# GpSimd subtracts low parts of weights in several pieces, and the planner's durations are refitted

## What is computed

```python
# layer 0: one input projection feeds two head groups
qa, ka, va, ga, qs, ks, vs, gs = split_cols(x @ w_in, EVEN_SPLITS)
# (A) 4 heads, differential attention: two softmax maps with a distance penalty
w = p[:, :, 0] - lam * p[:, :, 1]
# (B) 8 heads, stick-breaking attention
log_skip = jnp.where(earlier, jax.nn.log_sigmoid(-z), 0.0)
log_pass = lax.cumsum(log_skip, axis=3, reverse=True) - log_skip
a = jnp.where(earlier, jnp.exp(jax.nn.log_sigmoid(z) + log_pass), 0.0)
y = jnp.concatenate([ya, ys], axis=-1) @ w_out      # both gated by silu
# layer 1: (C) 8 heads of latent attention, low-rank q and kv, rotary part, gated, one output projection
# after each layer
h = layer_norm(ALPHA * h + y, ln_g[i], ln_b[i])
```

## Time and profile before

| what | value |
|---|---|
| median of 3 timed runs | 1339.77 us (1339.58 to 1344.28) |
| the profiled execution's own time | 1342.14 us |
| its span, first to last instruction | 1340.2 us |
| TensorE busy | 1294.9 us, 97% |
| VectorE busy | 871.3 us, 65% |
| ScalarE busy | 565.2 us, 42% |
| GpSimd busy | 477.1 us, 36%, 461 instructions |

### The profile page before, as it was taken

The page is one execution under the profiler, slowest core; times in us unless marked ns, Lnnn a source line. Parts: engine busy times, 40 slices in busy tenths (PEclk is TensorE's granted clock), DMA queues, the critical chain, the costliest instruction groups (busy, mean ns, idle before and its releaser), DMA issues.

```text
span 1340.2 us, 22174 instructions
## 1 busy us (share of the span) xinstructions
PE 1294.9 (97%) x8228; PEld 1221.5 (91%) x8228; DVE 871.3 (65%) x1959; ACT 565.2 (42%) x1332; POOL 477.1 (36%) x461
## 2 busy tenths in 40 slices
PE   8999999999999999998999999998999999999997
PEld 7999998999899999997888999998999989998886
DVE  5685868586677848669555323654778677776455
ACT  3444646364744535356101012533565545656200
POOL 3323221233224142246533324563333234334531
PEclk9999999999999999998999999999999999999999
DMA  6001010101010111214233311122111112115242
GB/s 227 33 28 36 17 49 32 49 33 48 33 40 25 37 45 52 63 29 137 68 126 126 111 32 61 66 83 75 36 48 45 48 44 64 41 46 194 69 161 79
DMA packets 46922, 88.25 MB, mean 66 GB/s; under 512 B 4048, under 2 KB 29648, under 8 KB 46688
## 3 DMA queue, kind: packets, MB, share of 16 engines
q1 hardware_dynamic: 44368, 78.45, 17.8%
q10 hardware_dynamic: 2448, 8.39, 1.6%
HBM read 66.84 MB, written 19.98 MB: 65 GB/s over the span
## 4 chain that ended last, share of the span: by engine, by line
PE 82%; DVE 9%; ACT 5%; issue 2%; POOL 1%; DMA 1%; DVEq 0%; SPq 0%; ACTq 0%; POOLq 0%
PE bank L2023 41%; PE bank L2174 13%; PE bank L2091 11%; PE bank L2146 8%; PE bank L2113 6%; DVE ring L1808 2%; DVE pb L1790 1%; PE bank L2062 1%; PE bank L2131 1%; ACT rtmp L1390 1%; DVE big L1607 1%; PE bank L2196 1%; DVE big L1847 1%; DVE tb L1737 1%; ACT vtok L1426 1%
## 5 line engine op out<-in xcount | busy, mean ns | idle before, releaser
L2023 PE MATMUL bank<-big,wsp 128*128 128x344 f32 (+2 forms) x3024 | 550.4, 327 | 8.4 <-DVE big L1607 4.5
L2023 PEld LDWEIGHTS bank<-big,wsp 128*128 128x128 f32 x3024 | 481.1, 189 | 15.0 <-POOL wsp L1067 4.2
L1066 POOL TENSOR_SCALAR wsp<-wraw 128x1024 fp32r<-128x1024 f32 (+4 forms) x92 | 84.3, 917 | 529.7 <-PE bank L2023 414.9
L1808 DVE TENSOR_TENSOR ring<-bank,ring 128x512 fp32r<-128x512 f32 (+3 forms) x280 | 154.9, 569 | 71.6 <-ACT ring L1477 44.8
L2174 PE MATMUL bank<-big,wsp 128*128 128x512 f32 x800 | 191.5, 397 | 1.5 <-DVE big L1847 1.2
L2174 PEld LDWEIGHTS bank<-big,wsp 128*128 128x128 f32 x800 | 149.3, 188 | 36.4 <-DVE big L1847 1.7
L1067 POOL TENSOR_TENSOR wsp<-wraw,wsp 128x1024 fp32r<-128x1024 f32 (+4 forms) x92 | 179.3, 1949 | 7.7
L2023 PE MATMUL bank<-h1t,wsp 128*128 128x344 f32 (+2 forms) x1080 | 173.9, 322 | 1.4 <-DVE lraw L1655 1.4
L2023 PEld LDWEIGHTS bank<-h1t,wsp 128*128 128x128 f32 x1080 | 170.2, 188 | 3.6 <-DVE lraw L1655 1.7
L1477 ACT ACTIVATE ring<-bank 128x512 fp32r<-128x512 f32 (+1 forms) x200 | 106.0, 555 | 112.8 <-PE bank L2113 80.4
L2146 PE MATMUL bank<-ring,vtok 128*128 128x256 f32 (+1 forms) x1040 | 143.3, 279 | 2.0 <-DVE ring L1808 1.0
(11 more groups left out here) (138 smaller groups left out, 1497.6 us busy)
## 6 DMA issues: line engine op xcount, KB each, us to landing
wraw<-in_w SPq DMA_DIRECT2D x47, 512.0 KB, 3.4
wraw<-y_scratch SPq DMA_DIRECT2D x17, 448.0 KB, 3.8
woraw<-in_wo SPq DMA_DIRECT2D x12, 512.0 KB, 5.3
y_scratch<-ot SPq DMA_DIRECT2D x37, 128.0 KB, 1.7
xres<-in_x SPq DMA_DIRECT2D x8, 512.0 KB, 4.7
h_scratch<-res ACTq DMA_DIRECT2D x8, 512.0 KB, 2.6
gate_scratch<-gtmp SPq DMA_DIRECT2D x8, 512.0 KB, 2.9
gate<-gate_scratch SPq DMA_DIRECT2D x8, 512.0 KB, 3.7
```

The source lines that it names most:

```text
L1066: pool.wait_ge(S["pool_step"], tick(nc.gpsimd.tensor_scalar(hi, raw, 1.0, 1.0, ALU.mult, ALU.mult)))
L1808: V.tensor_tensor(to, bank[T_BANK[t]][from_, 0:w], lo_hi(R[from_, r % NRING, 0, 0:w]), ALU.subtract)\
L2023: ins = mm(dst, wsp[:, SLOT[kind, u], a, k, :], rhs[:, b, k0 + k, c0:c0 + w], start=(k == 0 and a == 0 and b == 0), stop=last)
```

## The change

The subtraction in `split` gets a number of parts: as many as half the number of 128-column blocks of a weight tile, so 4 for 8 blocks, 3 for 7 (of 3, 3 and 1 blocks), 2 for 4 and 1 for 2. Nothing waits between the parts; the last one signals. The subtraction in GpSimd's `out_weight` goes in four parts of 256 columns. Other callers of `split` (latents, the last block of an output) keep one. In the planner, durations of the combination of kind A, of the scan of kind B, of products with a 128-column block, of GpSimd's split of a weight and of both kinds of low parts of output weights get other figures. Nothing else is edited.

```diff
@@ weave(layer)
             if kind == "A":
-                L.put("dve", "C", ("C", t), 1.9 * n_all + 1000, [("act", ("E", t, 1)), emptied(g)], 90)
+                L.put("dve", "C", ("C", t), 1.77 * n_all + 850, [("act", ("E", t, 1)), emptied(g)], 90)
...
             else:
-                L.put("dve", "C", ("C", t), 2.4 * n_all, [("act", s), emptied(g)], 90)
+                L.put("dve", "C", ("C", t), 2.15 * n_all + 60, [("act", s), emptied(g)], 90)
...
-            L.put("pe", "X", x, (1 if tiles == [0] else 2 if kind == "B" else 3) * (0.4545 * cols + 1.5 * len(tiles)),
+            L.put("pe", "X", x, (1 if tiles == [0] else 2 if kind == "B" else 3)
+                  * (pe_ns(cols) if tiles == [0] else sum(pe_ns(256) if tile <= pair_of(blocks)[0] + 1 else 83 for tile in tiles)),
...
-        L.put("pool", "W", ("W", n), 385 * kt + 450, ([("sp", ("LW", n))] if n >= first_w + 2 else []) + done, 20)
+        L.put("pool", "W", ("W", n), 385 * kt + 450 + 70 * (kt // 2 - 1), ([("sp", ("LW", n))] if n >= first_w + 2 else []) + done, 20)
...
-            L.put("dve", "W", wo, 2300, [("act", wo)], 90)
+            L.put("dve", "W", wo, 1700, [("act", wo)], 90)
         else:
-            L.put("pool", "O", wo, 2700, [("act", wo)], 20)
+            L.put("pool", "O", wo, 2800, [("act", wo)], 20)
@@ GpSimd
-            def split(hi, lo, raw):
+            def split(hi, lo, raw, parts=1):
 
                 pool.wait_ge(S["pool_step"], tick(nc.gpsimd.tensor_scalar(hi, raw, 1.0, 1.0, ALU.mult, ALU.mult)))
-                return nc.gpsimd.tensor_tensor(lo, raw, lo_hi(hi), ALU.subtract)
+                size = -(-raw.shape[1] // parts)
+                for a in range(0, raw.shape[1], size):
+                    b = min(a + size, raw.shape[1])
+                    ins = nc.gpsimd.tensor_tensor(lo[:, a:b], raw[:, a:b], lo_hi(hi[:, a:b]), ALU.subtract)
+                return ins
...
-                        ins = split(wsp[:, i % 2, 0, 0:kt, :], wsp[:, i % 2, 1, 0:kt, :], from_)
+                        ins = split(wsp[:, i % 2, 0, 0:kt, :], wsp[:, i % 2, 1, 0:kt, :], from_, max(kt // 2, 1))
...
-                nc.gpsimd.tensor_tensor(wok[:, 1, k, :], raw_out(layer, k), lo_hi(wok[:, 0, k, :]), ALU.subtract)\
-                    .then_inc(S["wo_split_pool"], 1)
+                for a in range(0, D, D // 4):
+                    part = slice(a, a + D // 4)
+                    ins = nc.gpsimd.tensor_tensor(wok[:, 1, k, part], raw_out(layer, k)[:, part], lo_hi(wok[:, 0, k, part]),
+                                                  ALU.subtract)
+                ins.then_inc(S["wo_split_pool"], 1)
```

## The result

The changed kernel takes 1354.05 us (median of 4 runs, 1352.45 to 1354.86) where the one before took 1340.02 in the same comparison: ratio 1.0097, 95% interval 1.0077 to 1.0116. I had forecast 1334.5. The profiled execution took 1352.45 us, with a span of 1350.5; it is the shortest of the four, while the profiled one of the kernel before (1342.14) is 2.1 us above its median, so the two profiles are 10.3 us apart where the medians are 14.0 apart.

A forecast was written before the change was run, and what follows sets the result against it. TensorE, busy 97%, was taken to bound the kernel. Terms -7.6 + 1.0 + 0.2 + 1.0 + 0.2 + 0 = -5.2 us gave 1336.9 profiled, 1334.5 us as median; range 1326 to 1345.

The forecast's parts named there:

- The bound: Whole kernel: TensorE, busy 97% of 1340.2 us, bounds it; 22 us idle in two attention stretches is the most to win.
- Pieces let VectorE in: At GpSimd's weight subtractions: a held VectorE step waits at most one piece, 0.77 us, where held 1.5 to 2.1 before.
- the waits on the combining: TensorE's waits on VectorE's combining of kind A (L1781): forecast to be gone.
- The price a piece: On GpSimd: 0.19 us for each of 218 more instructions, 41 us more busy time, near 518 us in all.
- The gain of -7.6: At TensorE's waits on held VectorE steps: three quarters of 10.1 us won, range 0 to -10.1.
- all eleven waits: TensorE waits from 55.92 to 1244.24 us whose last link is a VectorE step held by a GpSimd subtraction, 10.1 us.
- What GpSimd loses, +1.0 + 0.2 + 1.0: GpSimd's queue: query copies near 512 later +1.0, a 512-column weight in layer 1 +0.2, output weights +1.0 (0 to +2.9).
- my rival: Starved GpSimd, stick-breaking units: each piece waits out a scan, a subtraction needs 7 to 9 us; +8, 1348 us, chance 0.15.
- The start: First weight in pieces: TensorE starts 2.4 us later, then loses 2.2 us of later waits; net +0.2.
- the +0.2: Net cost in us forecast for the kernel's start, between -1.4 and +2.4.
- The refit, taken as 0 between -7 and +7: Planner's new durations alter only the order; effect taken as 0, bounded by a third of 22 us idle either way.
- -5.2: Sum of all forecast terms in us, on the profiled execution of 1342.14 us.

The follow-up runs named there:

- E1: Changed kernel with all planner durations, so the engines' order, as before and the pieces kept; 1347.18 us against 1342.26 for the kernel before, ratio 1.0040.
- the old order's three: Kernels alike in kind A's part: the one before, one with new planner figures in layer 1 only, one with the scan figure alone; idle 29.4, 27.5, 28.2 us.
- E2: Changed kernel with the new planner durations but every subtraction whole as before; 1355.68 us, ratio 1.0102.
- G2: Changed kernel with the planner's old duration for products put back (59.7 ns for 128 columns); 1354.45 us, ratio 1.0087.
- H1: Kernel before, whole subtractions, with only the planner's figure for combining of kind A refitted; 1351.99 us against 1341.70, ratio 1.0076.
- H1 to H4: Kernel before with planner figures changed: combining alone 1.0076, kind B's scan alone 1.0021, 128-column products alone 1.0020, VectorE's and TensorE's refits mirrored 1.0110.
- G4: Kernel before, no pieces, with old planner durations in layer 0 and the new ones in layer 1; 1340.06 us, ratio 0.9992.
- J1: Old planner durations in layer 0, new in layer 1; pieces for kind A's weights but the first and layer 1's attention and output; 1333.88 us against 1339.56, ratio 0.9951.
- G3: Old planner durations in layer 0, new in layer 1, and pieces only for kind A's weights but the first; 1338.21 us, ratio 0.9977.
- E3: Changed kernel with five early output-projection matmuls of layer 0 moved behind the turn of group 46, tile pair 1; 1351.69 us, ratio 1.0069.

## Why the prediction was wrong

**The bound** was read rightly: TensorE's idle time explains every kernel's span.

**Pieces let VectorE in**: right. The held step of 53 us, the cast of 810 and the scans' mean (2618 to 2464) came out as forecast. But the waits on the combining, which were to be gone, are 5.9 us where they were 2.5. The price a piece was too high: four back to back with nothing between take 2.84 us (at 26.31) where one takes 2.39, so 0.15 us for each further one and not 0.19; GpSimd is busy 533 us and not 518, and what was added (56 us) beyond 218 x 0.15 = 33 I take for waiting on VectorE, as the 6.14 us row shows it.

**The gain of -7.6** stood for all eleven waits. In kind A's part 3 to 4.5 us of it came, in either order (E1 against the old order's three, the change against E2: 32.6 and 37.1; G2 against H1: 36.0 and 39.1). In kind B's part it was more than eaten, and in layer 1 it came only with the new order.

**What GpSimd loses, +1.0 + 0.2 + 1.0**, is the first term that failed: in the old order the pieces cost 6.8 us net in kind B's part (E1). I had put +1.0 on query copies at one place (512) and +1.0 (0 to 2.9) on output weights; in that part the waits for these grew by 2.0 and 4.4 us, and those for weights, which I had at nothing there, by 2.5. It isn't my rival either, by which each piece waits out a scan and a subtraction needs 7 to 9 us: a 1024-column one takes 3.49 on average there and 4.8 at most. The sum of the pieces is +4.1 us of span where I had -5.2.

**The start** did no harm that shows: TensorE starts 1.5 us later (2.4 was expected) and loses its later waits. At the first turn of values the change (41.0 us) and E1 (40.4) are even ahead of the kernel before (41.7), but other kernels with whole subtractions are there at 39.0 to 40.4, so the +0.2 is neither shown nor refuted.
```profile
5.41 4.72 POOL L1071 TENSOR_TENSOR wsp<-wraw,wsp 128x256 fp32r<-128x256 f32 x4
...
10.18 10.33 PE L2031 MATMUL bank<-big,wsp 128*128 128x352 f32 x48 [4.23 <-POOL wsp L1071]
```

**The refit, taken as 0 between -7 and +7**, is the step that broke the forecast: by itself it is +13.0 us of span (E2; +13.7 by its ratio), outside its bounds. I bounded it by the idle time that was there, which bounds a gain only; a loss has no such bound. And I took it as equally likely to help or to hurt. H1 to H4 show that four orders near the old one, refitted or refitted backwards, are all slower in layer 0 taken whole. That fits an old order which happens to suit this chip better than its planner knows; why it does isn't settled, and four orders are few. That the new combining figure puts eight turns too early is seen (H1), not why the planner's picture is off there: in the change the combining before the wait at 225.45 itself took 2.0 us, less than the figure's 2.24 for its 784 keys.

**Their sum** is less than their parts: 4.1 and 13.0 give 17.1, the change has 10.3. By parts of the table, kind A's adds up (-4.5 and +7.7 against +3.2); the two overlap in kind B's, where +6.8 and +5.8 give +9.4, and in layer 1, where +1.3 and -0.5 give -2.9.

**TensorE's clock** is a rival that I left out: the same matmuls take longer where the granted clock is 0.50 (see the last section), and the change has 13.7 us at that clock in kind B's part, the kernel before 6.8. It doesn't explain the loss there by itself: with the same order and whole subtractions G4 has 3.4 us at 0.50 in this part, the kernel before and J1 6.8 and G3 10.2, and all four have 25.8 to 25.9 us of idle time. For the change, E1 (13.7 too) and E3 (17.1), no run separates the clock from the waits; nor does one in kind A's part.

## What to carry to other kernels

An order written by a planner is data that was matched to the chip: a change of its durations needs its own experiment, whatever it does for the fit of one instruction. Idle time bounds what a new order can gain, not what it can lose. Cutting a long instruction that blocks another engine pays where the blocked engine's work is short and waited for, and costs where that engine often has long work ready and its own result is waited for, since a piece may then wait out such an instruction; decide it stage by stage, with the idle time of equal work as the measure. A single large wait in the trace (8.9 us here) may hide others behind it: moving it brought 4 at most.

## What the runs showed of the hardware

GpSimd subtractions of 256 columns with no wait between them are recorded at 0.74 to 0.75 us each and 0.70 apart when nothing hinders them (four in 2.84 us), where one of 1024 takes 2.39, so most of the fixed cost of some 0.2 us stays. A waiting VectorE instruction of two SBUF inputs gets in at a boundary between two: in the change, three of them took 6.14 us with two scans between.

At a granted clock of 0.50 the same work takes longer. In E1 six score matmuls of 392 columns take 2.22 us behind a wait of 2.92 us, in a stretch at 0.51, and six more take 1.30 when the clock is back at 1.00:
```profile
348.71 2.22 PE L2098 MATMUL bank<-kst,qst 128*128 128x392 f32 x6 [2.92 <-POOL qst L1181]
...
352.10 1.30 PE L2098 MATMUL bank<-kst,qst 128*128 128x392 f32 x6
```
```profile
348.60:352.00 3.40, 3.29 (x12) 3.25 (x13) 0.08 (x1) 1.44 (x3) 0.05 (x1) 0.51 0.00 0
352.00:354.20 2.20, 2.20 (x15) 2.00 (x13) 0.54 (x1) 1.33 (x3) 0.00 (x0) 1.00 0.00 0
```

The record of TensorE's clock differs in the first microseconds where its pace does not. In the changed kernel the granted clock is 0.50 (1.2 GHz) after the wait of 4.23 us for the first weight, and 1.00 from 16 us; the stretches of 2 us hold 9 matmuls at 12 us and 15 at 16 us:
```profile
12.00:14.00 2.00, 2.00 (x9) 2.00 (x8) 1.72 (x2) 1.35 (x1) 0.00 (x0) 0.50 1.07 376
...
16.00:18.00 2.00, 2.00 (x15) 2.00 (x13) 0.25 (x1) 1.20 (x3) 0.58 (x1) 1.00 1.03 387
```
The kernel before is recorded at 1.00 throughout, with as few matmuls in a stretch at first:
```profile
12.00:14.00 2.00, 2.00 (x8) 2.00 (x8) 1.65 (x2) 1.35 (x1) 0.00 (x0) 1.00 1.06 380
```
So both start slowly (matmuls of 352 columns begin some 0.29 us apart at first, and 0.16 apart later), and the first projections cost about the same in each: 6.6 us from TensorE's start to the first key copy after (10.18 to 16.79), 6.9 before (8.70 to 15.56).
